# Identity multiplications on TensorE ahead of the front's last barrier and ahead of the first merged rows' turn

## What is computed

```python
z = rmsnorm(x, norm1) @ w_in          # q, k, v, forget logits, GLU input, memory queries, 3 gates
o_fox  = forgetting_attention(rmsnorm(q), rmsnorm(k), v, logf) @ w_fox_o     # 8 heads x 64
o_conv = conv_module(glu, hist) @ w_conv_o       # causal depthwise conv of width 31, LayerNorm, silu
o_mem  = cross_attention(rmsnorm(mq), mk, mv) @ w_mem_o                      # 4 heads x 128
merged = gates[0] * o_fox + gates[1] * o_conv + gates[2] * o_mem
x = x + merged @ w_out
x = x + peer(rmsnorm(x, norm2))       # top-16 product keys of 8 heads, gathers rows of two tables
```

## Time and profile before

| | us |
|---|---|
| runs | 3591.45, 3595.29, 3597.84; median 3595.29 |
| profiled execution, its own time | 3591.81 |
| profiled execution, span from first to last instruction | 3590.0 |
| TensorE (PE) busy | 3337.8 |
| VectorE (DVE) busy | 2886.5 |
| ScalarE (ACT) busy | 1525.5 |
| GpSimd (POOL) busy | 2086.6 |
| mean granted TensorE clock, share of full speed | 0.968 |

### The profile page before, as it was taken

The page is one execution under the profiler, slowest core; times in us unless marked ns, Lnnn a source line. Parts: engine busy times, 40 slices in busy tenths (PEclk is TensorE's granted clock), DMA queues, the critical chain, the costliest instruction groups (busy, mean ns, idle before and its releaser), DMA issues.

```text
span 3590.0 us, 46348 instructions
## 1 busy us (share of the span) xinstructions
PE 3337.8 (93%) x13366; PEld 2188.8 (61%) x13366; DVE 2886.5 (80%) x6788; ACT 1525.5 (42%) x3463; POOL 2086.6 (58%) x1831
## 2 busy tenths in 40 slices
PE   8999899989999997999799999999988899999987
PEld 7787655454443445676688888788864455655622
DVE  5499764167797987899999999998997798996765
ACT  5225576122442322233355555555543344544432
POOL 6222135046555665677767666676676766666675
PEclk9899999999999998999899999999998999999999
DMA  6415564698999999999999999999999999999999
GB/s 216 133 35 149 136 161 136 219 357 318 371 341 383 355 369 377 383 386 396 402 401 396 395 391 393 406 391 396 386 383 411 387 411 410 410 388 407 372 409 370
DMA packets 437898, 1215.03 MB, mean 338 GB/s; under 512 B 65203, under 2 KB 148311, under 8 KB 436752
## 3 DMA queue, kind: packets, MB, share of 16 engines
q0 software_dynamic: 239616, 872.52, 62.4%
q1 hardware_dynamic: 171738, 304.01, 24.4%
q10 hardware_dynamic: 26293, 35.54, 2.9%
HBM read 1124.32 MB, written 87.60 MB: 338 GB/s over the span
## 4 chain that ended last, share of the span: by engine, by line
PE 56%; DMA 13%; DVE 4%; issue 4%; POOL 3%; ACT 2%; SPq 0%; ACTq 0%; DVEq 0%; POOLq 0%
PE open_q_and_scores_ps L2831 17%; PE open_sums_ps L1940 8%; PE open_rows_ps L2915 5%; PE open_h_T_ps L1954 4%; DMA late_u_rows<-in_peer_v,late_kept_idx 4%; PE open_q_and_scores_ps L2889 3%; PE open_h_T_ps L2809 3%; DMA late_v_rows<-in_peer_v,late_kept_idx 3%; PE open_q_and_scores_ps L2762 3%; PE open_h_T_ps L2740 2%; PE open_sums_ps L2915 2%; DMA late_v_rows<-in_peer_v,table_twin_idx 2%; PE open_h_T_ps L2815 2%; PE open_sums_ps L2762 2%; POOL late_u_rows L2676 1%
## 5 line engine op out<-in xcount | busy, mean ns | idle before, releaser
L2689 POOL DMA_INDIRECT late_v_rows<-in_peer_v,late_kept_idx x573 | 550.7, 961 | 215.9 <-issue 133.8
L2676 POOL DMA_INDIRECT late_u_rows<-in_peer_u,late_kept_idx x320 | 481.9, 1506 | 261.0 <-DVE late_dots L3294 207.7
L3294 DVE CUSTOM_DVE_ANT_0 late_u_rows<-late_u_rows,open_rows_ps 128x1024 f32<-128x1024 f32 x432 | 521.6, 1209 | 13.8 <-DMA late_u_rows<-in_peer_u,late_expert_idx 6.9
L3329 DVE SCALAR_TENSOR_TENSOR late_x<-late_v_rows,late_weights,late_x 128x1024 f32<-128x1024 f32 x368 | 471.0, 1280 | 8.9 <-DMA late_v_rows<-in_peer_v,late_expert_idx 6.5
L2831 PE MATMUL open_q_and_scores_ps<-table_h_T_upper,table_u_T_upper 128*128 128x512 f32 x1024 | 423.8, 414 | 0.0
L2831 PE MATMUL open_q_and_scores_ps<-table_h_T_lower,table_u_T_upper 128*128 128x512 f32 x1024 | 402.2, 393 | 0.0
L2831 PE MATMUL open_q_and_scores_ps<-table_h_T_upper,table_u_T_lower 128*128 128x512 f32 x1024 | 401.1, 392 | 0.0
L2689 POOL DMA_INDIRECT late_u_rows<-in_peer_v,late_kept_idx x259 | 244.2, 943 | 118.9 <-issue 39.2
L1853 POOL DMA_INDIRECT open_u_rows<-in_peer_u,late_expert_idx x115 | 159.8, 1390 | 255.4 <-DVE late_dots L2287 128.9
L2915 PE MATMUL open_sums_ps<-late_v_rows,table_diag 128*128 128x512 f32 (+1 forms) x382 | 201.7, 643 | 62.8 <-DMA late_v_rows<-in_peer_v,table_twin_idx 33.9
L3039 ACT ACTIVATE table_u_T_upper<-open_h_T_ps 128x512 fp32r<-128x512 f32 x256 | 152.3, 595 | 208.0 <-PE open_h_T_ps L2809 208.0
(11 more groups left out here) (478 smaller groups left out, 8040.5 us busy)
## 6 DMA issues: line engine op xcount, KB each, us to landing
table_u_block<-in_peer_u SPq DMA_DIRECT2D x128, 512.0 KB, 7.2
scr_scores<-table_scores SPq DMA_DIRECT2D x32, 896.0 KB, 12.2
open_weight_columns<-in_w_in SPq DMA_DIRECT2D x64, 256.0 KB, 5.8
table_second_scores<-scr_scores SPq DMA_DIRECT2D x4, 4096.0 KB, 15.9
front_w_raw<-in_w_in SPq DMA_DIRECT2D x48, 256.0 KB, 5.1
table_first_scores<-scr_scores SPq DMA_DIRECT2D x3, 4096.0 KB, 16.5
scr_m<-open_gated SPq DMA_DIRECT2D x42, 256.0 KB, 6.1
late_v_rows<-in_peer_v,late_kept_idx POOLq DMA_INDIRECT x573, 9.5
```

The lines of the kernel that those rows point to most:

```text
L2676: pool.indirect_dma_start(u[k % U_RING][:], None, io["peer_u"][0], bass.IndirectOffsetOnAxis(ap=rows_of(n), axis=0)).then_inc(s_u[k % U_RI ...
L2689: pool.indirect_dma_start(slot[:], None, io["peer_v"][0], bass.IndirectOffsetOnAxis(ap=rows_of(m), axis=0)).then_inc(arrived, 16)
L3294: dve.tensor_tensor_reduce(u[k % U_RING][:], u[k % U_RING][:], h2_rows, 1.0, 0.0, ALU.mult, ALU.add, dots[:, n % COLS:n % COLS + 1]).then_ ...
L3329: dve.scalar_tensor_tensor(rows[:], slot[:], weight_of(m), rows[:], ALU.mult, ALU.add).then_inc(s_vsum, 1)
```

## The change

TensorE gets two stretches of identity multiplications. At the end of its part of the front it first waits as for a 69th group's bank 0 and then calls the helper with 55. In the opening, after the sixth gate logits, it waits until the memory product has been read and then does 14 of the same products into `pH`, before the turn of the merged rows.

```diff
 WARM = 8
+END_WARM, MERGE_WARM = 55, 14
...
                 for g in norm_groups[-TURN_LAG:]:
                     turn_norm(g)
+                bank_free(len(groups) + (-len(groups)) % NB)
+                keep_busy(END_WARM)
...
         gate_logits(4)
         gate_logits(5)
+        pe.wait_ge(s_used, S0 + 4)
+        for _ in range(MERGE_WARM):
+            pe.matmul(pH[:, 0, 0:P], c.ident[:], c.ident[:], start=True, stop=True)
         turn(O.m, (s_merged, S0 + 1), s_mturn)
```

## The result

The changed kernel took 3603.12 us (median of 20 runs, 3597.75 to 3607.11), the kernel before 3597.28 us (20 runs, 3591.29 to 3602.39): ratio 1.0018, 95% interval 1.0012 to 1.0025. The medians lie 5.8 us apart, with an interval of 4.3 to 9.0 us; forecast were 5.1.

What follows compares the result with a forecast made beforehand. PE was 93% busy, but the seam's front end was set by SP behind VectorE, and the projection lost 2.9 us to low clock. +7.6 - 0.4 - 2.1 = +5.1 us, forecast 3600 us on the median, range 3592 to 3607.

Steps and rivals of the forecast that it cites:

- Price of one multiplication: Both places: an identity multiplication, two records, takes 0.223 us at full clock and 0.43 at the low pace.
- The front: Before the attention: the 55 multiplications end PE's drain near 418.5 instead of SP's 410.9, costing +7.6 us.
- The single low spell: In the front: 3 multiplications at full pace to 405.1, 8 at the low one to 408.5, 44 at full.
- bounds of +6.0 and +9.4: Front's cost limits: +6.0 us with no low spell, +9.4 with one of 6.8 us.
- The barrier waits for PE: End of the front: PE replaces SP as last at the barrier, and nothing hides its overhang of +7.6 us.
- the free drain: Rival, chance 0.05: PE passes the front's barrier with its queue full, the front costs nothing, 3593 us on the median.
- the sleeping clock: Rival, chance 0.05: identity products do not wake the clock; front +16.6, merge +0.64, 3612 us on the median.
- the cheap product: Rival, chance 0.05: one multiplication takes 0.112 us, the 55 finish before SP, about 3593 us on the median.
- What a warm attention gives back: Attention's start at full clock: -0.4 us, bounds 0 and -4.6, as the second head's load caps it.
- The merge: Before the merged rows' turn: 14 multiplications overhang +0.64 us, the output projection speeds up by 2.75; sum -2.1 us.
- What follows moves along: After the output projection: residual, query and loads shift with it, nothing swallowing the merge's -2.1 us.
- The long spell: Rival, chance 0.20: front low spell of 6.8 us (+9.4), no attention gain, merge +0.64; +10.0, 3605 us on the median.

Runs made afterwards that it cites:

- E5: Changed kernel with 110 multiplications in the front and none at the merge: 3619.9 us, ratio 1.0072 to the kernel before.
- E1: Changed kernel with its 55 multiplications in the front but none at the merge: 3603.3 us, ratio 1.0021 to the kernel before.
- E9: Changed kernel with 20 in the front, 10 at the merge and 5 more between the seam's two barriers: 3596.9 us, ratio 1.0003 to the kernel before.
- E10: Changed kernel with none in the front and 10 at the merge: 3591.8 us, ratio 0.9990 to the kernel before.
- E2: Changed kernel with none in the front and its 14 at the merge: 3593.0 us, ratio 0.9993 to the kernel before.
- E8: Changed kernel with 20 and 10, the second head's queries and keys loaded ahead of both heads' values: 3600.3 us, ratio 1.0010 to the kernel before.
- E4: Changed kernel with counts fitted to the idle time, 20 in the front and 10 at the merge: 3592.7 us, ratio 0.9987 to the kernel before.
- E12: Changed kernel with 20 in the front and 10 at the merge, sampled a second time: 3593.6 us, ratio 0.9994 to the kernel before.
- E7: Changed kernel with 20 in the front and none at the merge: 3599.7 us, ratio 1.0012 to the kernel before.
- E11: Changed kernel with 20 in the front and none at the merge, sampled a second time: 3596.9 us, ratio 1.0002 to the kernel before.
- E6: Changed kernel with 55 split-type multiplications in the front instead of the helper's, none at the merge: 3602.0 us, ratio 1.0015 to the kernel before.

## Why the prediction was right

It forecast +5.1 us and named the part that loses and the part that gains; +5.8 was measured. The mechanism of the front holds, and it is the larger part by far. That the total came so near is in part luck: the traces add up to 6.5 us at the further units, since one term of the gain did not last, and the runs cannot tell 5.1 from 6.5. Step by step:

- *Price of one multiplication.* 0.223 us at full clock: E5 against E1 gives 0.222. It held because it was read from the helper's own two batches. (No record shows the clock granted at the first batch, and the windows print 1.00 there; but its pace of 0.21 us is that of the records at 0.50 in the front after.)
- *The front, +7.6 us.* Measured 7.8 (410.46 to 418.23). The single low spell came as foreseen, though from 403.9, ahead of the first multiplication: about 7 of the 55 ran at half pace, not 8, and none at full pace before them. (The prediction's bounds of +6.0 and +9.4 and its +16.6 leave out the last record's tail of 0.2 to 0.3 us, which changes nothing.)
- *The barrier waits for PE.* The drain did hold it, in every run that overshot; the rival of the free drain is out by E5, the sleeping clock by the windows after, the cheap product by the 14.02 us.
- *What a warm attention gives back, -0.4.* After the change the clock fell again 0.8 us into the attention, so the profile after could not test this. E9 did: -0.1. The bound of -4.6 us, which would have made the front cost 3 us instead of 7.6, was never approached. The reason was given as the load for attn_k_second, with ScalarE beside it. PE did wait longer for the load (0.89 us after, 0.91 in E9), but that took back only about 0.5 us; of the 3.0 us that E9's shorter spell could give, the greater part was out of reach because of the other engines, which the prediction gave one sentence. An attention at full clock throughout its first head was in no run.
- *The merge, -2.1.* Measured -2.2 from the last add to the residual: the projection 2.6 us shorter, the turn 0.3 us shorter at full clock, which the prediction had left out, and an overhang of 0.8 us. With 10 instead of 14 it is -2.8 (E10).
- *What follows moves along.* This missed one thing: the clock fell one pause later, and the first query lost 1.6 us, so that of the forecast 2.1 us only 0.6 was left at its end. It did so in the changed kernel, in E2 and in E8, but not in E4, E9, E10 and E12, so it depends on where the clock's steps lie in an execution; the count of 14 or 10 alone does not decide it (E8 has 10).
- *The long spell.* It was given 0.20. Its first part, a front spell of 6.8 us, was seen in E7; its three parts together in no profile. That the spell's place and length differ between executions of one kernel (E7 and E11) may be one source of the scatter of some 10 us among runs. Of the 14 us between the two profiled executions 6.0 stand at 950 us and the rest arose after that, in the late stages; no experiment was made on it.

Against the runs of before taken beside each, the changed kernel loses 5.8 us and E1, which has the front alone, 6.9. The 1.1 us between them is about what the traces say (6.5 and 7.3 at the further units), but each interval is 5 to 7 us wide, so the runs do not show that the merge gave anything back in the changed kernel.

## What to carry to other kernels

Work that only keeps TensorE's clock up has to end before the engine that comes last at the next barrier: price it by its own record spacing in the trace, against the slack between the two drains, and every multiplication beyond that is lost in full. In this kernel it paid only where TensorE's dense work follows at once and is itself the path, as the output projection is. Where the next stage is held by other engines and by loads issued behind the barrier, as the attention's first head is, a warm start bought next to nothing. And follow a gain past the next pause: the clock can fall there instead.

## What the runs showed of the hardware

Fifty-five 128-column multiplications of the split type ran 12 us without a gap in PE's records and the clock stayed at 1.2 GHz (E6), while with the float32 ones, two records each, it was back at 2.4 GHz 3.4 us after its fall in eight profiles and 6.8 us after it in one (E7). Why the two differ no run shows.

A record of the split type followed the last after 0.21 us at half clock (E6), the same as a float32 record of the same shape (0.214 in the first batch of the earlier trace rows). The Trainium skill ("TensorE: Matmul & The Clock Gate", Part 1) gives 107 ns for a cold matmul of 128 columns. The streams of E6 and of the helper took twice that, but a lone 128-column record can go at that pace: in the attention of the kernel before, at half clock, a score record read as the same type is followed after 0.11 us.

```profile
416.94 0.31 PE L1192 MATMUL attn_scores_ps<-first_k_T,first_q_T 128*128 128x128 f32 x1
...
417.05 0.41 PE L1193 MATMUL attn_scores_ps<-first_k_second,first_q_second 68*128 68x128 f32 x1
```

In E6 each record has a weight load of 0.333 us beside it. These loads may have been the pace there; that was not tried.
